# A two-block network on one core: the first product turned, two tiles at a time behind the norms, no GpSimd split beside the residuals, products whose result nobody reads, and an earlier evacuation of the projections

## The reference

```python
# first network: norms 0 to 3 (mixer, ffn, mixer, ffn)
h = rms_norm(x, norm_mix[0]); x = x + gdn_mixer(h, ...)    # norm 0; projections q k v z (6144 columns) and b, a (32 columns)
x = x + swiglu(rms_norm(x, norm_ffn[0]), w_gate_up, w_down) # norm 1; 2 x 2816 columns
x = x + mla_mixer(rms_norm(x, norm_mix[1]), ...)            # norm 2
x = x + swiglu(rms_norm(x, norm_ffn[1]), ...)               # norm 3
x = rms_norm(x, final_norm)
# second network, layers 0 and 1: norms 4, 5 and 6, 7
mod = silu(c) @ ada_w[l] + ada_b[l]; sh1, sc1, g1, sh2, sc2, g2 = split(mod)
h = rms_norm(x, norm1_g[l]) * (1 + sc1) + sh1
pa, pb, pc, pd = split(h @ w_in[l])
y = concat(rwkv7(pa), diff_attention(pb), spatial_gating(pc), forgetting_attention(pd))
x = x + g1 * (y @ w_out[l])
h = rms_norm(x, norm2_g[l]) * (1 + sc2) + sh2
x = x + g2 * conv_glu_ffn(h, ...)
```

## Time and profile before

| | before |
|---|---|
| median of 3 runs | 1665.9 us |
| lowest to highest | 1664.62 to 1670.54 us |
| the profiled run's own time | 1660.92 us |
| its span, first to last instruction | 1659.0 us |
| mean granted TensorE clock | 0.96 |
| TensorE busy | 1549.5 us (93%) |
| VectorE busy | 1074.0 us (65%) |
| ScalarE busy | 888.8 us (54%) |
| GpSimd busy | 417.1 us (25%) |
| read from memory | 272.57 MB, 165 GB/s over the span |

### The profile page before, as it was taken

The page is one execution under the profiler, slowest core; times in us unless marked ns, Lnnn a source line. Parts: engine busy times, 40 slices in busy tenths (PEclk is TensorE's granted clock), DMA queues, the critical chain, the costliest instruction groups (busy, mean ns, idle before and its releaser), DMA issues.

```text
span 1659.0 us, 35254 instructions
## 1 busy us (share of the span) xinstructions
PE 1549.5 (93%) x15256; PEld 1407.0 (85%) x15256; DVE 1074.0 (65%) x1782; ACT 888.8 (54%) x1456; POOL 417.1 (25%) x283
## 2 busy tenths in 40 slices
PE   7999998899999979999989889899998889989999
PEld 6888988779998867999878777799987778789987
DVE  3664464457779676677976666676746665676664
ACT  5654563455443555644456555566635664566652
POOL 1343362233434100344321320112301221012220
PEclk9999999999999999999989989899999996999999
DMA  6332210548889442788943202555451400445550
GB/s 242 138 103 79 79 52 25 209 144 323 313 327 366 139 178 77 289 322 323 359 154 120 83 29 80 225 178 178 168 175 60 144 27 28 188 154 170 191 186 26
DMA packets 40042, 275.88 MB, mean 166 GB/s; under 512 B 4560, under 2 KB 4688, under 8 KB 8528
## 3 DMA queue, kind: packets, MB, share of 16 engines
q1 hardware_dynamic: 39888, 273.63, 45.1%
HBM read 272.57 MB, written 1.05 MB: 165 GB/s over the span
## 4 chain that ended last, share of the span: by engine, by line
PE 81%; DVE 8%; ACT 6%; issue 2%; DMA 1%; POOL 1%; SPq 0%; ACTq 0%; POOLq 0%; DVEq 0%
PE ps L547 23%; PE ps L548 22%; PE ps L549 22%; PE ps L555 3%; PE ps L560 2%; DVE wl L535 1%; ACT wh L527 1%; DMA ring<-in_ws 1%; PE ps L2146 1%; DVE x_sb L2959 1%; DVE hTl L687 1%; PE ps L924 1%; POOL hTl L693 0%; ACT ps L734 0%; DMA cst<-in_cst 0%
## 5 line engine op out<-in xcount | busy, mean ns | idle before, releaser
L535 DVE TENSOR_TENSOR wl<-ring,wh 128x1024 fp32r<-128x1024 f32 (+3 forms) x364 | 459.0, 1266 | 342.8 <-ACT wh L527 341.8
L527 ACT ACTIVATE wh<-ring 128x1024 fp32r<-128x1024 f32 (+4 forms) x428 | 437.4, 1028 | 447.6 <-PE ps L549 439.4
L547 PE MATMUL ps<-hTh,wh 128*128 128x256 f32 x1904 | 553.2, 291 | 5.8 <-POOL hTl L693 3.0
L549 PE MATMUL ps<-hTh,wl 128*128 128x256 f32 x1904 | 544.7, 286 | 1.6 <-issue 1.6
L548 PE MATMUL ps<-hTl,wh 128*128 128x256 f32 x1904 | 543.4, 285 | 0.0
L547 PEld LDWEIGHTS ps<-hTh,wh 128*128 128x128 f32 x1904 | 367.0, 193 | 15.6 <-issue 13.8
L548 PEld LDWEIGHTS ps<-hTl,wh 128*128 128x128 f32 x1904 | 366.8, 193 | 0.2
L549 PEld LDWEIGHTS ps<-hTh,wl 128*128 128x128 f32 x1904 | 364.5, 191 | 0.0
L543 POOL TENSOR_TENSOR wl<-ring,wh 128x1024 fp32r<-128x1024 f32 x64 | 170.2, 2659 | 608.6 <-ACT wh L527 608.6
L1449 DVE SCALAR_TENSOR_TENSOR arena<-arena 128x1024 f32<-128x1024 f32 x96 | 158.0, 1663 | 1.0 <-DMA arena<-in_ws 1.0
L547 PE MATMUL ps<-wh,acts 128*128 128x512 f32 x366 | 145.2, 397 | 0.8 <-DVE wl L535 0.8
(11 more groups left out here) (464 smaller groups left out, 2152.0 us busy)
## 6 DMA issues: line engine op xcount, KB each, us to landing
ring<-in_ws SPq DMA_DIRECT2D x197, 1024.0 KB, 5.0
arena<-in_ws SPq DMA_DIRECT2D x48, 1024.0 KB, 8.2
ring<-in_ws SPq DMA_DIRECT2D x5, 768.0 KB, 4.5
ring<-in_ws SPq DMA_DIRECT2D x4, 512.0 KB, 3.6
ring<-in_ws SPq DMA_DIRECT2D x2, 780.0 KB, 4.2
rowt<-in_rowp SPq DMA_DIRECT2D x2, 610.0 KB, 4.1
x_sb<-in_x SPq DMA_DIRECT2D x2, 512.0 KB, 4.1
arena<-in_rowp SPq DMA_DIRECT2D x2, 512.0 KB, 4.6
```

Source lines behind the costliest of these rows:

```text
L527: ac.act(unit_hl(u)[0], unit_src(u), ACT.Copy).then_inc(*W.a(("hi", u)))
L535: ve.tt(l, unit_src(u), h, OP.subtract).then_inc(*W.v(("lo", u)))
L547: pe.mm(o_, lh, rh, start=start, stop=False)
L549: return pe.mm(o_, ll, rh, start=False, stop=stop)
```

## The change

Six things are done together.

- **Start.** The identity is a transfer of its own, second in the queue, and the transposes wait for it alone. The rest of the constants, the row and the positions go behind the third ring load. ScalarE takes a root of a constant first, ahead of its squares. `ba` is turned: the 32 columns are the fixed operand and 256 tokens the moving one, 24 matrix products into one bank; VectorE copies the 32x256 result, TensorE transposes it in two pieces, VectorE copies that to `ba`. The split of `ba`'s unit stands ahead of the k steps, that of the next unit behind k = 3.
- **Units.** In front of norms 1 to 7 no unit is GpSimd's. The low part of U+1 is VectorE's, as a step `late` behind the second scaling. Except at norm 2, units 1 and 2 change places, so that the first two units feed two different banks, and `two_T` does both for each k.
- **Unread products.** `stay_busy` puts products of 128x128 by 128x256 ahead of the second half's transposes, on the first unit's high part: 8 in norms 1 to 3, 16 in norms 4 to 7; norm 0 has 3 of 128x128 on the identity. They write a part of the bank that nobody reads and the transposes write afterwards.
- **Projections.** `pjv` of block b stands at `end_of[b] + pjo` in the weave, with `pjo` = -1.0 where it was +0.1.
- **Scalar products.** The step `dot` of `diff_attention` (the two sums, L2166 to L2174) is moved from among the projections to the stage of `pa` (`dot` = 2.0).
- **Zeroing.** GpSimd's zeroing of `krp` in front of norm 2's mixer waits for the modulation of the second network's first layer.

```diff
+    for name in ("f0u", "f1u", "win0", "f2u", "win1", "f3u"):
+        a, b = index[name, 1], index[name, 2]
+        units[a], units[b] = units[b], units[a]
+        index[name, 1], index[name, 2] = b, a
+        la, lb = units[b].load, units[a].load
+        loads[la].units, loads[lb].units = [a - 1, b], [a, b + 1]
     for name in ("f0u", "mi0", "f1u", "win0", "f2u", "win1", "f3u"):
-        units[index[name, 1]].pool, units[index[name, 2]].pool = True, False
+        u = index[name, 0]
+        units[u + 1].pool, units[u + 2].pool, units[u + 1].late = False, False, True
...
-                    yield u
+                    yield ("late", u) if UNITS[u].late else u
...
+        def two_T(pe, u, os, kt, rh, rl, come):
+
+            for i in range(2):
+                pe.wait_ge(*lo_done(u + i))
+            for k in range(kt):
+                for c in come(k):
+                    pe.wait_ge(*c)
+                m = [mm3(pe, os[i], unit_hl(u + i)[0][:, k, :], unit_hl(u + i)[1][:, k, :], rh(k), rl(k), k == 0, k == kt - 1) for i in range(2)]
+            for i in range(2):
+                m[i].then_inc(*W.t(("used", u + i)))
...
+                ac.wait_ge(*N.v[0, "pre"])
+                ac.act(small[:, 11:12], small[:, 10:11], ACT.Sqrt).then_inc(*N.a((n, "pre")))
...
+        def stay_busy(pe, n):
+
+            o_ = psum[NBANKS[n][0]].rearrange("p (a b) -> p a b", b=256)[:, :, 128:256]
+            if n == 0:
+                for i in range(3):
+                    pe.mm(o_[:, 0, :], C["ident"], C["ident"], start=True, stop=True)
+                return
+            u = UIX[("", "f0u", "mi0", "f1u", "win0", "f2u", "win1", "f3u")[n], 0]
+            pe.wait_ge(*W.a["hi", u])
+            w = wh[u % NUNIT]
+            for i in range(8 if n < 4 else 16):
+                pe.mm(o_, w[:, 0:128], w[:, 0:256].rearrange("p (a b) -> p a b", b=128), start=True, stop=True)
...
-                    pe.wait_ge(*DMA["cst"]["cst"])
+                    pe.wait_ge(*DMA["idn"]["idn"])
+                if t:
+                    stay_busy(pe, n)
...
-            unit_tok(pe, UIX["ba", 0], [psum[4][:, 0:32], psum[5][:, 0:32]], 0, 8, 8, h_, l_, h_come(0))
+            tile_T(pe, UIX["ba", 0], psum[4][0:32, 0:256], 8, h_, l_, h_come(0))
...
+            ve.cp(gcT[0:32, :], psum[4][0:32, 0:256]).then_inc(*GP.v("baT"))
+            yield "Tout"
+            ve.wait_ge(*GP.t["ba"])
+            ve.cp(ba, psum[5][:, 0:64].rearrange("p (t n) -> p t n", t=2)).then_inc(*GP.v("ba"))
+
+        def bav_t(pe):
+            yield "T"
+            pe.wait_ge(*GP.v["baT"])
             for t in range(2):
-                ve.cp(ba[:, t, :], psum[4 + t][:, 0:32]).then_inc(*GP.v(("ba", t)))
+                m = tr(pe, psum[5][:, 32 * t:32 * t + 32], gcT[0:32, 128 * t:128 * t + 128])
+            m.then_inc(*GP.t("ba"))
...
-                tile_T(pe, UIX[f"f{s}u", m], psum[UB[i % 4]][:, 256 * (m % 2):256 * (m % 2) + 256], 8, h_, l_, h_come(n) if m == 0 else None)
+                if m == 0:
+                    two_T(pe, UIX[f"f{s}u", 0], [psum[UB[j]][:, 0:256] for j in range(2)], 8, h_, l_, h_come(n))
+                elif m != 2:
+                    tile_T(pe, UIX[f"f{s}u", m], psum[UB[i % 4]][:, 256 * (m % 2):256 * (m % 2) + 256], 8, h_, l_)
...
-                tile_T(pe, UIX[f"win{l}", m], psum[4 + m // 2][:, 256 * (m % 2):256 * (m % 2) + 256], 8, h_, l_, h_come(4 + 2 * l) if m == 0 else None)
+                if m == 0:
+                    two_T(pe, UIX[f"win{l}", 0], [psum[4 + j][:, 0:256] for j in range(2)], 8, h_, l_, h_come(4 + 2 * l))
+                elif m != 2:
+                    tile_T(pe, UIX[f"win{l}", m], psum[4 + m // 2][:, 256 * (m % 2):256 * (m % 2) + 256], 8, h_, l_)
...
-            yield "lam"
+            yield "dot"
...
-                    of(nt, [("mean", 1)] * (n != 4) + [("sqrt", 1), ("scale", 1), ("T", 1)]) + of(nt, [("k", k) for k in range(8)]) + [[("fill", U + 2)]])
-
-        plan_ = of("n0", [("sq", 0), ("mean", 0), ("sqrt", 0), ("scale", 0), ("T", 0), ("sq", 1), ("mean", 1), ("sqrt", 1), ("scale", 1), ("T", 1)])
-        plan_ += of("n0", [("k", k) for k in range(8)]) + of("ba", [0])
+                    of(nt, [("mean", 1)] * (n != 4) + [("sqrt", 1), ("scale", 1)]) + [[("w", ("late", U + 1))]] + of(nt, [("T", 1)]) + of(nt, [("k", k) for k in range(8)]) + [[("fill", U + 2)]])
+
+        ba0 = UIX["ba", 0]
+        plan_ = of("n0", ["pre", ("sq", 0), ("mean", 0), ("sqrt", 0), ("scale", 0), ("T", 0), ("sq", 1), ("mean", 1), ("sqrt", 1), ("scale", 1), ("T", 1)])
+        plan_ += [[("fill", ba0)]] + of("n0", [("k", k) for k in range(4)]) + [[("fill", ba0 + 1)]] + of("n0", [("k", k) for k in range(4, 8)]) + of("ba", [0])
...
-            plan_ += weave((0, pjs), *[(end_of[b] + 0.1, of(f"pjv{l}", [b])) for b in range(5)],
+            plan_ += weave((0, pjs), *[(end_of[b] + T0["pjo"], of(f"pjv{l}", [b])) for b in range(5)],
...
+                    if loaded[0] == 3:
+                        ORDER.append(("late", "consts"))
...
+        def late_s(sp):
+            yield "consts"
+            sp.dma(rowt[:, 0:1056], A["rowp"][:, 0:1056].to_broadcast([128, 1056])).then_inc(*DMA["row"]("row"))
+            sp.dma(cst[:, 128:], A["cst"][:, 128:]).then_inc(*DMA["cst"]("cst"))
+            sp.dma(posi[:, :], A["posi"]).then_inc(*DMA["pos"]("pos"))
...
+            sp.dma(x3[:, 0, :], xs[:, 0, :]).then_inc(*DMA["x0"](0))
+            sp.dma(cst[:, 0:128], A["cst"][:, 0:128]).then_inc(*DMA["idn"]("idn"))
+            sp.dma(x3[:, 1, :], xs[:, 1, :]).then_inc(*DMA["x1"](1))
```

More of the change, by code:

```diff
@@ L258, in __init__ @@
     def __init__(self, load, view, pool):
-        self.load, self.view, self.pool = load, view, pool
+        self.load, self.view, self.pool, self.late = load, view, pool, False
 def weight_units(offs):
@@ L417, in build_program @@
         DMA = {k: Signal(sem(f"landed_{k}"), 16) for k in
-               ("x0", "x1", "col", "cst", "row", "pos", "row_l0", "row_l1", "misc0", "misc1", "ada0", "ada1", "ada2", "cond", "out")}
+               ("x0", "x1", "idn", "col", "cst", "row", "pos", "row_l0", "row_l1", "misc0", "misc1", "ada0", "ada1", "ada2", "cond", "out")}
         RING = [Signal(sem(f"landed_ring{i}"), 16) for i in range(NSLOT)]
@@ L664, in norm_v @@
             xn = arena[:, at:at + 2048]
+            if n == 0:
+                yield "pre"
+                ve.zero(small[:, 10:11], 1.0).then_inc(*N.v((0, "pre")))
             for t in range(2):
@@ L3074, in build_program @@
             (0, 0.5, [[(f"p{n}", (2 * i + j, k))] for n, i in PAIRS for j in range(2) for k in range(2)]), (48, 0.5, of("go", halves(16 - TAIL))),
-            (2, [[("bav", "out")]]), (3, of("gt", range(11))),
+            (1, of("bav", ["out", "T", "Tout"])), (3, of("gt", range(11))),
             *[(2 * at + d, of("cv", [st])) for at, (n, i) in enumerate(PAIRS) if n != "z" for d, st in ((2.01, ("c", i + 8 * (n == "v"))), (2.02, i + 8 * (n == "v")), (3.3, ("s", i + 8 * (n == "v"))))],
@@ L3209, in sync @@
             xs, os_ = (ap.rearrange("(t p) n -> p t n", p=128) for ap in (A["x"], out))
-            for t in range(2):
-                sp.dma(x3[:, t, :], xs[:, t, :]).then_inc(*DMA[f"x{t}"](t))
+            sp.dma(x3[:, 0, :], xs[:, 0, :]).then_inc(*DMA["x0"](0))
+            sp.dma(cst[:, 0:128], A["cst"][:, 0:128]).then_inc(*DMA["idn"]("idn"))
+            sp.dma(x3[:, 1, :], xs[:, 1, :]).then_inc(*DMA["x1"](1))
             sp.dma(colt[:, :], A["colp"]).then_inc(*DMA["col"]("col"))
-            sp.dma(cst[:, :], A["cst"]).then_inc(*DMA["cst"]("cst"))
-            sp.dma(rowt[:, 0:1056], A["rowp"][:, 0:1056].to_broadcast([128, 1056])).then_inc(*DMA["row"]("row"))
-            sp.dma(posi[:, :], A["posi"]).then_inc(*DMA["pos"]("pos"))
-            follow(ORDER, {"ring": ring_s(sp), "adal": ada_s(sp), "rows": rows_s(sp)})
+            follow(ORDER, {"ring": ring_s(sp), "late": late_s(sp), "adal": ada_s(sp), "rows": rows_s(sp)})
             for t, n in PIECES:
```

17 lines of the change are left out of this document (11 added, 6 removed).

## The result

| | before | changed |
|---|---|---|
| median | 1665.26 us (1663.69 to 1670.54, 4 runs) | 1643.93 us (1640.39 to 1650.17, 4 runs) |
| ratio to before | 1 | 0.9872, 95% interval 0.9846 to 0.9898 |
| the profiled run's own time, and its span | 1660.92, 1659.0 us | 1640.39, 1638.6 us |
| mean granted clock | 0.960 | 0.966 |

A forecast was written before the change was run, and what follows sets the result against it. TensorE, busy for 93% of the span, was taken as the bound, so gains had to come from its idle or slow stretches. 9.5 + 18 + 0 + 11 - 0.5 = 38 us took the median from 1665.9 to 1628, range 1617 to 1645.

The forecast's parts named there:

- A, the start: Kernel start: earlier identity and table load, and 24 products in place of 48, gain 9.5 us, bounds 7 and 11.
- The table load: At the start, on ScalarE between squares and root: moving it ahead of the squares saves its 1.28 us.
- The wide products begin that much earlier: At the start: `ba` ends at 17.6, so q's wide products begin 8.7 us before the old 26.35.
- B, norms 4 to 7: No GpSimd split (5.7 us) and shorter stretches with the clock held (12.3): 18 us, upper bound 20.
- Rival (1): The clock falls at norms 4 to 7 all the same: 7 us there, sum 27, time 1639; chance 0.14.
- C, norms 1 to 3: Unread products fit the wait and pairs offset the late split: zero, bounds 0.6 us lost and 0.5 won.
- D, the projections: Earlier copies out of the bank shorten TensorE's waits in both layers: 11 us, bounds 4 and 16.
- Rival (2): The projections' wait only moves to the late transfer or RWKV chain: 4 us there, time 1635; chance 0.10.
- The long wait: Projections: waits of 5.3 and 4.5 us for the copy shrink to about 0.75 each, so 8.3 us go.
- The short waits are 1.8 and 2.1: Projections: the shorter copy waits also end one split earlier; half taken, 2.0 us gained.
- The sum: Whole kernel: the terms add up to 38 us, taking the median from 1665.9 to 1628.
- (4): Whole kernel: the change leaves all stretches as they are and the start hides behind transfers; time 1665, chance 0.02.

The follow-up runs named there:

- no_unread: The changed kernel without the unread products at norms 1 to 7, those of norm 0 kept; 1648.21 us, ratio 0.9924 to the kernel before.
- norms_only: The kernel before with only the change's part at norms 1 to 7; 1646.51 us, ratio 0.9898 to the kernel before.
- copy4: The changed kernel plus 31 idle TensorE instructions, with block 3's projection copy ordered 4 steps before its end instead of 1; 1632.79 us, ratio 0.9794 to before.
- pad95: The changed kernel with 95 idle instructions in TensorE's queue ahead of the first transposes; 1642.20 us, ratio 0.9852 to the kernel before.
- pad159: The changed kernel with 159 idle instructions in TensorE's queue ahead of the first transposes; 1649.70 us, ratio 0.9913 to the kernel before.
- pool_split: The changed kernel with unit U+1 split by GpSimd again, pairs and unread products kept; 1657.95 us, ratio 0.9941 to the kernel before.

## Why the prediction was right or wrong

- **A, the start, 9.5 forecast, 0 measured (by the interval from 3 won to 3 lost).** Within the start the first product came 0.3 us later than forecast and the first wide one 1 us earlier, since the products ran at the upper clock from the first. The table load was worth its 1.28 us and no more: in before's trace the operation behind it starts 1.29 us after it, at 7.20. The step that failed is the sentence "The wide products begin that much earlier", with nothing behind it on whether they also end earlier. The mechanism in its place: TensorE's instructions arrive in blocks of 256, and removing 31 moved the dense products against the blocks. With the place restored the term is 8.5 us (5.5 to 11.5), so its size was right.
- **B, norms 4 to 7, 18 forecast, 16.6 measured.** Right, by its own steps: 0.69, 1.29 of idle time (about 1 forecast), transposes 1.09, 9.25 to the split (8.8 forecast). The clock was not held everywhere: 0.89 at norm 5, and a fall of 3.4 us at two of the four norms. The unread products took 2.16 instead of 1.9. Rival (1), the clock falls all the same, came true in part, and its price was too high: in no_unread, where the clock fell for 6.8 us behind each norm, 12.1 stay and not the 5.7 to 7. That two tiles for each step shorten the stretch at either clock would explain it; this is argued, not shown.
- **C, norms 1 to 3, 0 forecast.** By the nearest splits around them in the changed kernel's trace they gave 0.2, 0.8 and 0.2, in norms_only's 0.2 each. So about 1, slightly above its upper bound of 0.5.
- **D, the projections, 11 forecast, about 3 measured, which the intervals do not tell from nothing.** Rival (2) was nearest: the wait moved, though neither to the late transfer nor to the RWKV chain but to the next copy. The long wait went nearly as forecast (5.3 to 1.3, where 0.75 was to stay), and the step that failed is "The short waits are 1.8 and 2.1; the copies that end them also stand one split earlier; I take half": they grew to 4.6 and 4.4. It was read which wait goes, not who waits when TensorE comes 4 us sooner to the same queue. The 5.1 us that the table shows between marks 241 and 261 are luck of that execution: in the seven others with the earlier copy in the plan (copy4 aside) the lead fell there by 1.5 to 5.3 us.
- **The sum.** 0 + 17 + 1 + 3 = 21. The range held because its upper end was taken from the rivals (1) and (2) and the scatter; of the rivals only (4) let the start's gain go, by another way and with all the rest. So that the time lies in the range is partly luck. (Added up, the bounds of the terms give 1618 to 1638 rather than 1617 to 1637; nothing hangs on this.) What the clock does among the mixers and whether the small terms are noise stays open: between marks 241 and 261 single executions differ by up to 10 us, from kernels that are alike there.

## What to carry to other kernels

A lead at the start of a program is worth nothing until it has passed every stage: put a mark into each stage that both versions share, and look where it is lost. Where TensorE has hundreds of small products in a row, count its instructions: adding or removing a few dozen ahead of them cost and gave 8 us here, as much as the whole start, so compare versions at the same count modulo 256, or try a shift before an edit is judged. And where one wait is removed, ask what the waiting engine reaches next and what stands in front of that on the engine it will wait for.

## What the runs showed of the hardware

- TensorE waits for its own instructions in dense runs of small products: 0.3 to 3.2 us a time, at one place of each 256, 5 to 16 us in the first mixer. The Trainium skill ("Runtime: NRT & Kernel Launch", section "Instruction fetch mechanics") describes refilling in blocks of 16 KB or 256 instructions, with which the traces agree, and says that the cost of crossing a block is mostly hidden, because instructions are issued slower than they are fetched. Here it was not: 256 instructions were used up in 1.1 us, the waits ended 2.2 to 2.8 us after a transfer began, and 31 idle instructions changed the kernel by 8.6 us.
- An instruction that only waits for what is already there took TensorE 0.108 us (95 and 159 of them in a row, pad95 and pad159).
- Products whose result nobody reads, put into a wait that stays, kept the clock up for longer: at norm 5 1.29 us of idle time ahead of the transposes and clock 0.89, against 3.20 us and 0.79; behind norms 4 to 7 together 6.8 us at 1.2 GHz against 27.
- A VectorE operation of 128x512 float32 with two SBUF operands took 0.69 us alone and 2.12 to 2.18 beside GpSimd's split of a unit (norms 4 to 7 of before and of pool_split).
